# The last feed-forward product of a one-core encoder kernel, as seven Strassen block products instead of eight plain ones

## The chip, the core and the metric

The kernel runs on one core of one Trainium2 chip, in float32. The metric is the time of one execution on the device in microseconds (us); less is better. TensorE multiplies, VectorE (DVE in the rows), ScalarE (ACT) and GpSimd (POOL) do the elementwise work, and transfers between HBM and the core's memory are issued by queues: SyncE (SP) issues the weight loads and the stores, GpSimd a few others.

## The reference

One encoder layer on 512 tokens of width 1024 (no loop over layers: `DEPTH` is 1): three token mixers, their gated sum, and a gated feed-forward network. What matters here is the end:

```python
x = x + merged @ w_out[l]
h = rmsnorm(x, norm_ffn[l])
gu = h @ ffn_w_gate_up[l]                    # 1024 -> 2 * 2816
x = x + (silu(gu[..., :D_FF]) * gu[..., D_FF:]) @ ffn_w_down[l]   # 2816 -> 1024
return rmsnorm(x, final_norm)
```

## The kernel before, in words

The program is written by hand, one instruction stream for each engine, with semaphores between them; no scheduler moves anything. A float32 product is made from three faster ones: every operand is rounded to a `hi` part (by ScalarE, type float32r), the rest `lo` = operand - `hi` is made by VectorE, and `product` (lines 913 to 915) issues `hi*hi`, `hi*lo` and `lo*hi` into the same PSUM bank. A bank holds 128x512 results; there are eight.

Weights come in blocks in the order of the list `weight_blocks`, each up to 128 x 2048 elements (1 MB). A block passes three stages: SyncE loads it into one of three `w_raw` buffers (line 681, after `w_lo_done` says that the block three ahead has been split), ScalarE rounds it into one of two `w_hi` buffers once TensorE has used the block two ahead (`consumed`), and VectorE writes the rest into `w_lo` (line 1998 is VectorE's tensor_tensor helper, line 1544 ScalarE's activation helper). On ScalarE and VectorE this preparation is the call `prep(after(block))` at the place where TensorE works on `block`: it prepares the next one.

The stages around the change, in order of time:

- the gates and branch products, 12 + 12 blocks, from about 450 to 648; then `merged @ w_out`, four blocks `("wo", half, kk)`. GpSimd issues one transfer for the residual `x1` when the last branch block is done (line 893); VectorE's `residual` waits for it (`x1_landed`) and stands ahead of the preparation of the fourth `w_out` block.
- gate and up, 22 blocks `("gu", f)` for 128 features each, 48 matmuls a block. The weight is the stationary operand, `hT_hi` and `hT_lo` the moving one. ScalarE takes silu of the gate bank, VectorE multiplies it with the up bank, in PSUM; ScalarE rounds the result to `act_hi` and VectorE writes `act_lo`.
- the last product, 12 blocks `("down", half, f0)`: for each half of 512 output columns, over 22 feature tiles f, four token tiles t. The activation is stationary (128x128), the weight moves (512 columns). A half fills four banks, so the second half's products run while VectorE adds the first half into `x1` (`add_glu`).
- the tail: ScalarE sums squares of each 512 columns of `x1`, VectorE makes the reciprocal root, GpSimd multiplies `x1` with the final norm's weights (line 902), ScalarE and VectorE scale two token tiles each, SyncE stores.

GpSimd has nothing to do between the scan's last operation (`r_tok`, line 829) and the `x1` transfer but wait.

## Time and profile before

| | |
|---|---|
| median of 3 runs | 1077.66 us (1075.33 to 1756.04) |
| the profiled execution | 1073.17 us |
| its span, first to last instruction | 1071.4 us |
| granted TensorE clock, mean over the span | 0.992 of full |
| TensorE busy | 1036.9 us (97%) |
| VectorE busy | 521.4 us (49%) |
| ScalarE busy | 379.2 us (35%) |
| GpSimd busy | 138.1 us (13%) |
| moved by transfers | 87.18 MB, 81 GB/s over the span |

Busy time is the sum of an engine's instructions. TensorE's matmuls overlap each other, so the length of one is not the interval between two. The second part of the page cuts the span into 40 slices of 26.8 us; each digit is a share in tenths. The profile attributes an idle stretch to what ended it ("<-PE psum" is: the semaphore came from a matmul that wrote psum). "The order" below is the list of an engine's instructions as they stand in the program, with no times in it.

### The profile page before, as it was taken

What the parts mean: (1) busy time and instruction counts of PE and PEld (TensorE: products, weight loads), DVE (VectorE), ACT (ScalarE), POOL (GpSimd) and SP (SyncE); (2) the same over time, 40 slices, a digit from 0 to 9 for tenths busy, and PEclk for the clock granted to TensorE, in tenths of its full rate; (3) what the DMA queues carried; (4) which work ended last, traced back from release to release, by engine and by line L of the source; (5) the groups of instructions that cost most, each with busy time, mean ns of one, the idle gap of its engine ahead of it and who ended that gap; (6) DMA issues with size and microseconds to landing.
All of it is one profiled execution on the core that took longest, in us unless ns stands there. A gap on an engine that the chain in (4) does not pass through costs nothing.

```text
span 1071.4 us, 14260 instructions
## 1 busy us (share of the span) xinstructions
PE 1036.9 (97%) x5850; PEld 863.5 (81%) x5850; DVE 521.4 (49%) x731; ACT 379.2 (35%) x567; POOL 138.1 (13%) x208
## 2 busy tenths in 40 slices
PE   8999999999989998999999999899999999999995
PEld 6889889866678887888888888788888888888884
DVE  6775546477666778455152525543233333322313
ACT  6545645754432221633232312343232322221312
POOL 4010001436763221000000000000000000000201
PEclk9999999999999999999999999999999999999998
DMA  9431230000100014123232336222433333233201
GB/s 301 132 109 58 79 98 2 1 4 9 21 12 2 2 40 133 45 76 102 78 118 86 95 118 214 79 79 79 115 82 108 89 97 100 83 114 116 87 13 79
DMA packets 101856, 87.18 MB, mean 81 GB/s; under 512 B 12117, under 2 KB 90401, under 8 KB 101792
## 3 DMA queue, kind: packets, MB, share of 16 engines
q1 hardware_dynamic: 100144, 81.80, 25.2%
q0 software_dynamic: 1488, 4.40, 1.1%
q8 instruction: 47, 0.77, 0.3%
q14 instruction: 17, 0.14, 0.0%
q10 hardware_dynamic: 160, 0.07, 0.0%
HBM read 83.64 MB, written 2.62 MB: 81 GB/s over the span
## 4 chain that ended last, share of the span: by engine, by line
PE 93%; DVE 4%; issue 1%; ACT 1%; DMA 1%; POOL 0%; SPq 0%; DVEq 0%; POOLq 0%; ACTq 0%
PE psum L913 24%; PE psum L914 24%; PE psum L915 24%; PE psum L1232 2%; PE psum L1239 1%; PE psum L1252 1%; PE psum L1331 1%; PE psum L1387 1%; PE psum L1206 1%; PE psum L1375 1%; PE psum L1304 1%; PE psum L1361 1%; PE psum L1192 1%; PE psum L1126 1%; DVE Xm L1998 1%
## 5 line engine op out<-in xcount | busy, mean ns | idle before, releaser
L1998 DVE TENSOR_TENSOR w_lo<-w_raw,w_hi 128x2048 fp32r<-128x2048 f32 (+3 forms) x81 | 166.9, 2060 | 232.2 <-ACT w_hi L1544 232.1
L913 PE MATMUL psum<-hT_hi,w_hi 128*128 128x512 f32 x704 | 275.2, 391 | 1.0 <-DVE hT_lo L2042 1.0
L914 PE MATMUL psum<-hT_lo,w_hi 128*128 128x512 f32 x704 | 274.4, 390 | 0.0
L915 PE MATMUL psum<-hT_hi,w_lo 128*128 128x512 f32 x704 | 274.2, 390 | 0.0
L1544 ACT ACTIVATE w_hi<-w_raw 128x2048 fp32r<-128x2048 f32 (+3 forms) x82 | 140.8, 1718 | 159.7 <-PE psum L915 147.5
L913 PEld LDWEIGHTS psum<-hT_hi,w_hi 128*128 128x128 f32 x704 | 132.6, 188 | 28.7 <-issue 1.2
L915 PEld LDWEIGHTS psum<-hT_hi,w_lo 128*128 128x128 f32 x704 | 132.4, 188 | 27.5
L914 PEld LDWEIGHTS psum<-hT_lo,w_hi 128*128 128x128 f32 x704 | 132.4, 188 | 27.3
L1998 DVE TENSOR_TENSOR psum<-gate_act,psum 128x512 f32<-128x512 f32 x22 | 15.3, 696 | 120.4 <-PE psum L915 120.4
L913 PE MATMUL psum<-w_hi,act_hi 128*128 128x512 f32 x176 | 68.5, 389 | 0.0
L914 PE MATMUL psum<-w_lo,act_hi 128*128 128x512 f32 x176 | 68.5, 389 | 0.0
L915 PE MATMUL psum<-w_hi,act_lo 128*128 128x512 f32 x176 | 68.5, 389 | 0.0
L1544 ACT ACTIVATE act_hi<-psum 128x512 fp32r<-128x512 f32 x22 | 13.2, 600 | 122.6 <-DVE psum L1998 122.6
L2088 DVE SCALAR_TENSOR_TENSOR dnT<-psum,vcol,dnT 128x510 f32<-128x510 f32 (+1 forms) x48 | 35.9, 749 | 13.6 <-ACT dnT L1544 12.1
L1544 ACT ACTIVATE p_tok<-psum,smax 128x512 f32<-128x512 f32 (+1 forms) x48 | 29.5, 615 | 32.7 <-DVE smax L2321 24.6
L1544 ACT ACTIVATE sig<-psum 128x512 f32<-128x512 f32 x24 | 14.0, 599 | 76.3 <-PE psum L915 76.3
L915 PEld LDWEIGHTS psum<-w_hi,act_lo 128*128 128x128 f32 x176 | 33.0, 188 | 6.9
L913 PEld LDWEIGHTS psum<-w_hi,act_hi 128*128 128x128 f32 x176 | 33.0, 188 | 6.9
L914 PEld LDWEIGHTS psum<-w_lo,act_hi 128*128 128x128 f32 x176 | 33.0, 188 | 6.7
L896 POOL DMA_DIRECT2D fin_w<-in_final_norm_dram x1 | 0.5, 541 | 291.9 <-PE psum L915 291.9
L913 PE MATMUL psum<-oT_hi,w_hi 128*128 128x512 f32 x96 | 37.3, 389 | 0.0
L914 PE MATMUL psum<-oT_lo,w_hi 128*128 128x512 f32 x96 | 37.3, 389 | 0.0
(315 smaller groups left out, 1596.3 us busy)
## 6 DMA issues: line engine op xcount, KB each, us to landing
w_raw<-in_ffn_w_gate_up_dram SPq DMA_DIRECT2D x44, 512.0 KB
w_raw<-in_w_in_dram SPq DMA_DIRECT2D x21, 1024.0 KB
w_raw<-in_ffn_w_down_dram SPq DMA_DIRECT2D x10, 1024.0 KB
w_raw<-in_w_out_dram SPq DMA_DIRECT2D x4, 1024.0 KB
x_tok<-in_x_dram SPq DMA_DIRECT2D x4, 512.0 KB, 5.1
w_raw<-in_mem_w_kv_dram SPq DMA_DIRECT2D x2, 1024.0 KB
w_raw<-in_w_branch_mla_dram SPq DMA_DIRECT2D x4, 512.0 KB
w_raw<-in_w_branch_dn_dram SPq DMA_DIRECT2D x4, 512.0 KB
```

The costliest lines, as they stand in the source:

```text
L913: pe.matmul(o, s_hi, m_hi, start=first, stop=False)
L914: pe.matmul(o, s_hi, m_lo, start=False, stop=False)
L915: return pe.matmul(o, s_lo, m_hi, start=False, stop=last)
L1126: m = pe.transpose(bank(key, QK)[:, j * P:(j + 1) * P], qk_tok[:, t % 2, h * QK:(h + 1) * QK], ident[:, :])
L1192: pe.matmul(bank(key), lhs_rows[q, d, :], rhs_rows[q, d, p, :, :].rearrange("p j n -> p (j n)"), start=True, stop=True).then_inc(full(key), 1)
L1206: m = pe.matmul(bank(key)[:, j * P:(j + 1) * P], dnT[half, 4 + j, t * P:(t + 1) * P], rhs, start=True, stop=True)
L1232: pe.matmul(bank(key), qT[:, h, t * P:(t + 1) * P], kT[:, h, :], start=True, stop=True).then_inc(full(key), 1)
L1239: m = pe.transpose(bank(key)[:, k * P:(k + 1) * P], p_tok[:, n % 2, k * P:(k + 1) * P], ident[:, :])
L1252: m = pe.matmul(out[u * DV:(u + 1) * DV, :], v_mla[:, k, (h0 + u) * DV:(h0 + u + 1) * DV], pT4[(n + u) // 2 % 2][:, (n + u) % 2, k * P:(k ...
L1544: return nc.scalar.activation(o, i, f, **kw)
L1998: return dve.tensor_tensor(o, a, b, op)
L2088: ins = dve.scalar_tensor_tensor(out=dnT[:, ct, a:b], in0=bank(key)[:, a + s:b + s], scalar=vcol[:, c:c + 1], in1=dnT[:, ct, a:b], op0=ALU ...
```

## The change

Cut the activations A (512 tokens x 2816 features) and the weights W (2816 x 1024) into halves: A11, A12 / A21, A22 and W11, W12 / W21, W22. Eight block products make A @ W. Strassen's form makes it with seven (M1 to M7) from sums and differences of quarters; every factor is a quarter, or a sum or difference of two quarters, and VectorE adds or subtracts the seven products into `x1`.

- **Product.** 22 steps instead of 12 blocks. A step s < 11 takes feature tiles i and i + 11 and does four products (M1, M4, M7, M5) of 256 x 128 x 512, 24 matmuls; a step s >= 11 does three (M2, M3, M6), 18 matmuls. The last two steps go product by product, not step by step. Each M has two banks. The second three use banks 0 to 5, those of M1, M4 and M7.
- **Weight quarters.** Of the seven factors two are plain quarters, one is a difference made by VectorE in the loaded buffer (`step_difference`), and four are sums `w_sum` that exist in HBM: GpSimd copies all of `ffn_w_down` (11.53 MB) to `w_sum` with four transfers HBM to HBM, waits for them, then adds quarters to it with eight transfers that accumulate into their destination, 1.44 MB each. SyncE waits for all eight before the first step's load.
- **Activations.** They are no longer split as they come: VectorE writes the product of gate and up in float32 to `acts`, GpSimd makes five differences for each pair of feature tiles (`pair_sums`), ScalarE rounds four or three factors a step to one of three `a_hi` buffers, VectorE writes `a_lo`. The second and third of these buffers lie on `hT_hi` and `hT_lo`, so they can be written only after the last gate/up product.
- **Order.** Gate/up tiles come as 0, 11, 1, 12, ... (`GU_ORDER`). The final adds are `take(m, row, half, op, step)`: each bank is added to or subtracted from one or two quarters of `x1`, 24 adds instead of 8. GpSimd's final-norm load moves ahead in its queue (`fin_w` lies on used activations).

The core of the diff:

```diff
+NP = NF // 2
+GU_ORDER = [i + NP * u for i in range(NP) for u in range(2)]
+STEPS = 2 * NP
+FINAL = [(half, 2 * row + t) for half, row in ((0, 0), (0, 1), (1, 0), (1, 1)) for t in range(2)]
+SUM_PARTS = 8
+FIRST_FOUR, LAST_THREE = (1, 4, 7, 5), (2, 3, 6)
...
+        acts = v("acts", [P, NP, 7, 256], 0)
+        sums_at = [(v0 + 77 * KB), hbase + 12 * KB, hbase + 20 * KB]
+        a_hi = [at(f"a_hi{i}", [P, 4, 256], F32R, o) for i, o in enumerate(sums_at)]
+        a_lo = [at(f"a_lo{i}", [P, 4, 256], F32R, o + 4 * KB) for i, o in enumerate(sums_at)]
+        dw = [at(f"dw{i}", [P, 4, 512], F32, ring + 8 * KB * ((len(blocks) + i) % RAW)) for i in range(RAW)]
+        late = lambda i: acts[:, i, 3:7, :].rearrange("p a b -> p (a b)")
+        y_out = [late(t) for t in range(NT)]
+        fin_w, square4 = late(NT), late(NT + 1)
...
+        def step_in(s):
+            return (w_hi[(NB + s) % 2], w_lo[(NB + s) % 2], a_hi[s % 3], a_lo[s % 3])
+
+        def step_landed(eng, s):
+            eng.wait_ge(dw_landed[s % 3], 16 * sum(3 if i < NP else 2 for i in range(s % 3, s + 1, 3)))
+
+        def step_free(eng, s):
+            if s < 2:
+                filled(eng, ("u", GU_ORDER[NF - 2 + s]))
+            elif s - 2 == NP - 1:
+                filled(eng, ("M", FIRST_FOUR[-1], 1))
+            else:
+                eng.wait_ge(step_used, s - 1 - (s - 2 > NP - 1))
+
+        factors = lambda s: 4 if s < NP else 3
...
+            upper, lower = (slice(0, D_FF // 2), slice(D_FF // 2, D_FF))
+            left, right = slice(0, 512), slice(512, D)
+            in_steps = lambda a, r: a[r, :].rearrange("(i p) n -> i p n", p=P)
+            w_top, w_low = in_steps(ffn_w_down[0], upper), in_steps(ffn_w_down[0], lower)
+            s_top, s_low = in_steps(w_sum, upper), in_steps(w_sum, lower)
+            sp.wait_ge(sum_ready, 16 * SUM_PARTS)
+            for s in range(STEPS):
+                if s < RAW:
+                    sp.wait_ge(w_lo_done, NB - RAW + 1 + s)
+                else:
+                    sp.wait_ge(dw_lo, s - RAW + 1)
+                i, slot, landed = s % NP, dw[s % 3], dw_landed[s % 3]
+                sp.dma_start(slot[:, 0, :], w_top[i, :, left]).then_inc(landed, 16)
+                if s < NP:
+                    sp.dma_start(slot[:, 3, :], w_low[i, :, right]).then_inc(landed, 16)
+                pair = (s_low if s < NP else s_top)[i, :, :].rearrange("p (u n) -> p u n", u=2)
+                sp.dma_start(slot[:, 1:3, :], pair).then_inc(landed, 16)
...
+            for c in range(4):
+                r = slice(D_FF // 4 * c, D_FF // 4 * (c + 1))
+                pool.dma_start(w_sum[r, :], ffn_w_down[0][r, :]).then_inc(sum_begun, 16)
+            pool.wait_ge(sum_begun, 16 * 4)
+            for c in range(SUM_PARTS // 4):
+                top = slice(D_FF // 4 * c, D_FF // 4 * (c + 1))
+                low = slice(D_FF // 2 + top.start, D_FF // 2 + top.stop)
+                left, right = slice(0, 512), slice(512, D)
+                for dst_r, dst_c, src_r, src_c in ((low, left, top, left), (low, right, low, left), (top, left, top, right),
+                                                   (top, right, low, right)):
+                    pool.dma_start(w_sum[dst_r, dst_c], ffn_w_down[0][src_r, src_c], accum_op=ALU.add).then_inc(sum_ready, 16)
+
             consumed(pool, index[("br", 3, 2)])
             pool.dma_start(x1[:, :, :], x[0].rearrange("(t p) d -> p t d", p=P)).then_inc(x1_landed, 16)
 
-            consumed(pool, index[("gu", NF - 1)])
...
+            def pair_sums(i):
+                for u in range(2):
+                    released(pool, ("u", i + NP * u))
+                a = lambda n: acts[:, i, n, :]
+                pool.tensor_tensor(a(4), a(0), a(3), ALU.subtract).then_inc(act_sums, 1)
+                pool.tensor_tensor(a(5), a(1), a(0), ALU.subtract).then_inc(act_sums, 1)
+                pool.tensor_tensor(a(6), a(1), a(3), ALU.subtract).then_inc(act_sums, 1)
+                pool.wait_ge(act_sums, 5 * i + 3)
+                pool.tensor_tensor(a(1), a(2), a(3), ALU.subtract).then_inc(act_sums, 1)
+                pool.wait_ge(act_sums, 5 * i + 4)
+                pool.tensor_tensor(a(2), a(2), a(0), ALU.subtract).then_inc(act_sums, 1)
+
+            for i in range(NP):
+                pair_sums(i)
+            pool.wait_ge(a_lo_done, NT + 1)
+            pool.dma_start(fin_w, final_norm.partition_broadcast(P)).then_inc(fin_landed, 16)
...
+            def down_product(s, m, a_unit, w_unit):
+                wh, wl, ah, al = step_in(s)
+                c = slice(512 * w_unit, 512 * w_unit + 512)
+                first, last = s % NP == 0, s % NP == NP - 1
+                for t in range(2):
+                    key = ("M", m, t)
+                    if first:
+                        claim(pe, key)
+                    r = slice(t * P, (t + 1) * P)
+                    ins = product(bank(key), ah[:, a_unit, r], al[:, a_unit, r], wh[:, c], wl[:, c], first, last)
+                    if last:
+                        ins.then_inc(full(key), 1)
+                return ins
+
+            def step_ready(s):
+                pe.wait_ge(dw_lo, s + 1)
+                pe.wait_ge(a_lo_done, s + 1)
+
+            for s in range(STEPS - 2):
+                step_ready(s)
+                for m, a_unit, w_unit in ((1, 1, 0), (4, 0, 1), (7, 3, 2), (5, 2, 3)) if s < NP else ((2, 1, 0), (3, 0, 2), (6, 2, 1)):
+                    ins = down_product(s, m, a_unit, w_unit)
+                if s != NP - 1:
+                    ins.then_inc(step_used, 1)
+            for m, a_unit, w_unit in ((2, 1, 0), (3, 0, 2), (6, 2, 1)):
+                for s in (STEPS - 2, STEPS - 1):
+                    if m == 2:
+                        step_ready(s)
+                    down_product(s, m, a_unit, w_unit)
...
+            def step_rounded(s):
+                wh, _, _, _ = step_in(s)
+                n = factors(s)
+                step_free(act, s)
+                step_landed(act, s)
+                if s < NP:
+                    act.wait_ge(dw_diff, s + 1)
+                A(wh[:, 0:512 * n], dw[s % 3][:, 0:n, :].rearrange("p a b -> p (a b)")).then_inc(dw_hi, 1)
...
+            for s in range(1, STEPS):
+                step_rounded(s)
+                if s == 1:
+                    acts_rounded(s)
+                acts_rounded(s + 1)
...
+            def step_difference(s):
+                if s < NP:
+                    step_landed(dve, s)
+                    d = dw[s % 3]
+                    tt(d[:, 0, :], d[:, 0, :], d[:, 3, :], ALU.subtract).then_inc(dw_diff, 1)
+
+            def acts_rest(s):
+                _, _, ah, al = step_in(s)
+                n, first = factors(s), 3 if s < NP else 0
+                dve.wait_ge(a_hi_done, s + 1)
+                tt(al[:, 0:n, :], acts[:, s % NP, first:first + n, :], f32(ah[:, 0:n, :]), ALU.subtract).then_inc(a_lo_done, 1)
+
+            def step_rest(s):
+                wh, wl, _, _ = step_in(s)
+                n = factors(s)
+                dve.wait_ge(dw_hi, s + 1)
+                tt(wl[:, 0:512 * n], dw[s % 3][:, 0:n, :].rearrange("p a b -> p (a b)"), f32(wh[:, 0:512 * n]),
+                   ALU.subtract).then_inc(dw_lo, 1)
...
+            for s in range(1, STEPS):
+                if s == NP + 1:
+                    take(1, 0, 0, ALU.add, x1_added)
+                    take(1, 1, 1, ALU.add, None)
+                    taken(1)
+                    take(4, 0, 0, ALU.add, x1_added)
+                    take(4, 1, 0, ALU.add, None)
+                    taken(4)
+                    take(7, 0, 0, ALU.add, None)
+                acts_rest(s)
+                step_difference(s + 1)
+                step_rest(s)
+                if s == NP + 2:
+                    taken(7)
+                    take(5, 0, 0, ALU.subtract, x2_ready)
+                if s == NP + 3:
+                    take(5, 0, 1, ALU.add, None)
+            taken(5)
+            take(2, 1, 0, ALU.add, x2_ready)
+            take(2, 1, 1, ALU.subtract, None)
+            taken(2)
+            take(3, 0, 1, ALU.add, x2_ready)
+            take(3, 1, 1, ALU.add, None)
+            taken(3)
+            take(6, 1, 1, ALU.add, x2_ready)
             final_means(0)
```

Three places of the order, row by row as it is printed. First VectorE at the turn from gate and up to the last product, before (`w_lo0` and `w_lo1` are the two buffers, numbers behind names are memory locations; a block of weights is 128x2048, the fifth of a half 128x2048 and the sixth 128x1024):

```order
L1998 TENSOR_TENSOR psum<-gate_act_56,psum 128x512 [waits bank_free2,bank_full3]
L1998 TENSOR_TENSOR act_lo_165<-psum,act_hi_164 128x512 [waits glu_hi]
L1998 TENSOR_TENSOR w_lo0_87<-w_raw1_83,w_hi0_85 128x2048 [waits w_hi_done]
L1998 TENSOR_TENSOR w_lo1_88<-w_raw2_84,w_hi1_86 128x2048 [waits w_hi_done]
L1998 TENSOR_TENSOR w_lo0_87<-w_raw0_82,w_hi0_85 128x2048 [waits w_hi_done]
L1998 TENSOR_TENSOR w_lo1_88<-w_raw1_83,w_hi1_86 128x2048 [waits w_hi_done]
L1998 TENSOR_TENSOR w_lo0_87<-w_raw2_84,w_hi0_85 128x1024 [waits w_hi_done]
```

and now (`dw0` to `dw2` are the loaded steps, `a_lo` the rests of the activations; the first four rows behind the first `acts` belong to steps 0 and 1):

```order
L2102 TENSOR_TENSOR acts_164<-gate_act_56,psum 128x2x256 [waits bank_free0,bank_full1]
L2102 TENSOR_TENSOR dw0_171<-dw0_171 128x512 [waits dw_landed0]
L2102 TENSOR_TENSOR dw1_172<-dw1_172 128x512 [waits dw_landed1]
L2102 TENSOR_TENSOR a_lo0_168<-acts_164,a_hi0_165 128x1024 [waits a_hi_done]
L2102 TENSOR_TENSOR w_lo1_88<-dw0_171,w_hi1_86 128x2048 [waits dw_hi]
L2102 TENSOR_TENSOR acts_164<-gate_act_56,psum 128x2x256 [waits bank_free2,bank_full3]
L2102 TENSOR_TENSOR a_lo1_169<-acts_164,a_hi1_166 128x1024 [waits a_hi_done]
L2102 TENSOR_TENSOR dw2_173<-dw2_173 128x512 [waits dw_landed2]
L2102 TENSOR_TENSOR w_lo0_87<-dw1_172,w_hi0_85 128x2048 [waits dw_hi]
L2102 TENSOR_TENSOR a_lo2_170<-acts_164,a_hi2_167 128x1024 [waits a_hi_done]
L2102 TENSOR_TENSOR dw0_171<-dw0_171 128x512 [waits dw_landed0]
L2102 TENSOR_TENSOR w_lo1_88<-dw2_173,w_hi1_86 128x2048 [waits dw_hi]
```

Ahead of each step's weight rest there now stand the rest of its activations and the difference of the next step, and the last gate/up product (the second `acts` row) stands between the work of step 0 and that of step 1. Second, VectorE in the middle of the product, where banks are emptied while TensorE goes on into others, before:

```order
L1998 TENSOR_TENSOR w_lo1_88<-w_raw0_82,w_hi1_86 128x2048 [waits w_hi_done]
L1998 TENSOR_TENSOR x1_161<-x1_161,psum 128x512 [waits bank_full0]
L1998 TENSOR_TENSOR x1_161<-x1_161,psum 128x512 [waits bank_full1]
L1998 TENSOR_TENSOR x1_161<-x1_161,psum 128x512 [waits bank_full2]
L1998 TENSOR_TENSOR x1_161<-x1_161,psum 128x512 [waits bank_full3]
L1998 TENSOR_TENSOR w_lo0_87<-w_raw1_83,w_hi0_85 128x2048 [waits w_hi_done]
```

and now, behind the weight rest of step 11:

```order
L2102 TENSOR_TENSOR x1_161<-x1_161,psum 128x512 [waits bank_full0]
L2102 TENSOR_TENSOR x1_161<-x1_161,psum 128x512 [waits bank_full1]
L2102 TENSOR_TENSOR x1_161<-x1_161,psum 128x512 [waits bank_full0]
L2102 TENSOR_TENSOR x1_161<-x1_161,psum 128x512 [waits bank_full1]
L2102 TENSOR_TENSOR x1_161<-x1_161,psum 128x512 [waits bank_full2,bank_free1,bank_free0]
L2102 TENSOR_TENSOR x1_161<-x1_161,psum 128x512 [waits bank_full3]
L2102 TENSOR_TENSOR x1_161<-x1_161,psum 128x512 [waits bank_full2]
L2102 TENSOR_TENSOR x1_161<-x1_161,psum 128x512 [waits bank_full3]
L2102 TENSOR_TENSOR x1_161<-x1_161,psum 128x512 [waits bank_full4,bank_free3,bank_free2]
L2102 TENSOR_TENSOR x1_161<-x1_161,psum 128x512 [waits bank_full5]
L2102 TENSOR_TENSOR a_lo0_168<-acts_164,a_hi0_165 128x768 [waits a_hi_done]
L2102 TENSOR_TENSOR w_lo1_88<-dw0_171,w_hi1_86 128x1536 [waits dw_hi]
```

Four adds with a 2048-column rest on either side have become ten, ahead of the activations' rest and the weight rest of step 12. Third, GpSimd's queue behind the scan, before:

```order
L829 TENSOR_TENSOR r_tok<-v_tok,dg 128x512 [waits bank_full7]
L829 TENSOR_TENSOR r_tok<-v_tok,dg 128x512 [waits bank_full4]
L893 DMA x_161<-in_x_dram 128x4x1024 [waits bank_full7]
L896 DMA fin_w<-in_final_norm_dram 128x1024 [waits bank_full3]
L902 TENSOR_TENSOR y_out<-x_161,fin_w 128x512 [waits x2_ready,fin_landed]
L902 TENSOR_TENSOR y_out<-x_161,fin_w 128x512 [waits x2_ready] x7
```

and now:

```order
L875 TENSOR_TENSOR r_tok<-v_tok,dg 128x512 [waits bank_full7]
L875 TENSOR_TENSOR r_tok<-v_tok,dg 128x512 [waits bank_full4]
L940 DMA w_sum<-in_ffn_w_down_dram 64x11264 x4
L948 DMA w_sum<-in_ffn_w_down_dram 704x512 [waits sum_begun]
L948 DMA w_sum<-in_ffn_w_down_dram 704x512 x7
L951 DMA x_161<-in_x_dram 128x4x1024 [waits bank_full7]
L957 TENSOR_TENSOR acts<-acts 128x256 [waits bank_free3,bank_free1]
L958 TENSOR_TENSOR acts<-acts 128x256
L959 TENSOR_TENSOR acts<-acts 128x256
L961 TENSOR_TENSOR acts<-acts 128x256 [waits act_sums]
L963 TENSOR_TENSOR acts<-acts 128x256 [waits act_sums]
```

The twelve new transfers and the wait between them stand between the scan and the transfer of `x1`, in the same queue; the copies are described as 64 rows of 11264 elements, the sums as 704 rows of 512.

## Rows read from the trace of the kernel before

**Rows 1.** The page, parts 1 and 2: busy time, and the granted clock.

```profile
PE 1036.9 (97%) x5850; PEld 863.5 (81%) x5850; DVE 521.4 (49%) x731; ACT 379.2 (35%) x567; POOL 138.1 (13%) x208
...
PEclk9999999999999999999999999999999999999998
```

**Rows 2.** The page, part 5: group | busy us, mean ns | idle before.

```profile
L913 PE MATMUL psum<-w_hi,act_hi 128*128 128x512 f32 x176 | 68.5, 389 | 0.0
```

**Rows 3.** Timeline of TensorE: start us, length us, engine, line, operation; last product.

```profile
951.46 0.39 PE L913 MATMUL psum<-w_hi,act_hi 128*128 128x512 f32 x1
...
1060.03 0.39 PE L915 MATMUL psum<-w_hi,act_lo 128*128 128x512 f32 x1
```

**Rows 4.** Windows: stretch, its length, busy time per engine, PEclk, DMA share, GB/s.

```profile
core 0: us, PE busy (x) PEld busy (x) DVE busy (x) ACT busy (x) POOL busy (x), PEclk, DMA share, GB/s
...
697.00:935.00 238.00, 238.00 (x1051) 197.65 (x1050) 84.58 (x72) 70.75 (x73) 0.00 (x0) 0.99 0.33 93
935.00:1056.00 121.00, 121.00 (x536) 100.19 (x535) 27.21 (x18) 24.72 (x23) 7.65 (x5) 1.00 0.22 74
```

**Rows 5.** Timelines of ScalarE and VectorE at the second block of the last product.

```profile
951.72 1.92 ACT L1544 ACTIVATE w_hi<-w_raw 128x2048 fp32r<-128x2048 f32 x1 [7.81 <-PE psum L915]
...
953.67 2.29 DVE L1998 TENSOR_TENSOR w_lo<-w_raw,w_hi 128x2048 fp32r<-128x2048 f32 x1 [7.43 <-ACT w_hi L1544]
```

**Rows 6.** Groups by form, 400 to 1072: VectorE, then ScalarE.

```profile
L1998 DVE TENSOR_TENSOR w_lo<-w_raw,w_hi 128x2048 fp32r<-128x2048 f32 x50 | 114.6, 2292 | 135.3 <-ACT w_hi L1544 135.3
L1998 DVE TENSOR_TENSOR w_lo<-w_raw,w_hi 128x1024 fp32r<-128x1024 f32 x14 | 17.2, 1226 | 80.2 <-ACT w_hi L1544 80.2
...
L1998 DVE TENSOR_TENSOR x<-x,psum 128x512 f32<-128x512 f32 x16 | 10.7, 684 | 17.0 <-PE psum L915 17.0
...
L1544 ACT ACTIVATE w_hi<-w_raw 128x2048 fp32r<-128x2048 f32 x50 | 95.5, 1910 | 122.4 <-PE psum L915 110.2 <-DVE attT L1998 12.2
L1544 ACT ACTIVATE w_hi<-w_raw 128x1024 fp32r<-128x1024 f32 x14 | 14.8, 1058 | 33.7 <-PE psum L915 33.7
```

**Rows 7.** Groups by form of GpSimd, whole span.

```profile
L902 POOL TENSOR_TENSOR y_out<-x,fin_w 128x512 f32<-128x512 f32 x8 | 12.2, 1544 | 108.7 <-DVE x L1998 108.5
...
L800 POOL TENSOR_TENSOR block_in<-block_fb 128x256 f32<-128x256 f32 x2 | 1.7, 853 | 0.2
```

**Rows 8.** Timeline of VectorE in the tail.

```profile
1060.46 0.69 DVE L1998 TENSOR_TENSOR x<-x,psum 128x512 f32<-128x512 f32 x1 [0.60 <-PE psum L915]
1061.07 0.16 DVE L2029 RECIPROCAL small<-small 128x2 f32<-128x2 f32 x1
1061.26 1.45 DVE L1998 TENSOR_TENSOR small<-small 128x2 f32<-128x2 f32 x2
...
1063.64 0.36 DVE L1998 TENSOR_TENSOR small<-small 128x2 f32<-128x2 f32 x2
```

**Rows 9.** Timeline of GpSimd: its last operations of the scan.

```profile
406.14 2.48 POOL L829 TENSOR_TENSOR r_tok<-v_tok,dg 128x512 f32<-128x512 f32 x2
```

**Rows 10.** Windows: the stretch in which `x1` and a block of w_out land.

```profile
650.00:655.00 5.00, 5.00 (x24) 4.14 (x23) 3.17 (x3) 2.06 (x2) 0.00 (x0) 1.00 1.04 400
```

**Rows 11.** Timeline of GpSimd, then issues: KB each, us from issue to landing.

```profile
648.27 0.83 POOL L893 DMA_DIRECT2D x<-in_x_dram  x1 [239.66 <-PE psum L915]
...
x<-in_x_dram POOLq DMA_DIRECT2D x1, 2048.0 KB, 11.0
```

**Rows 12.** Transfers issued: KB each, us from issue to landing.

```profile
mem_tok<-in_mem_dram POOLq DMA_DIRECT2D x1, 1024.0 KB, 6.2
```

**Rows 13.** Timeline of the queue of SyncE, 405 to 430.

```profile
406.25 19.86 SPq L681 DMA_DIRECT2D w_raw<-in_w_in_dram  x4
```

**Rows 14.** Timelines of VectorE and ScalarE at the first gate block.

```profile
444.95 2.28 DVE L1998 TENSOR_TENSOR w_lo<-w_raw,w_hi 128x2048 fp32r<-128x2048 f32 x1
...
450.89 1.91 ACT L1544 ACTIVATE w_hi<-w_raw 128x2048 fp32r<-128x2048 f32 x1
```

**Rows 15.** Timelines of ScalarE and VectorE at the blocks of w_out.

```profile
658.95 1.92 ACT L1544 ACTIVATE w_hi<-w_raw 128x2048 fp32r<-128x2048 f32 x1 [6.89 <-PE psum L915]
...
671.78 2.29 DVE L1998 TENSOR_TENSOR w_lo<-w_raw,w_hi 128x2048 fp32r<-128x2048 f32 x1 [1.32 <-ACT w_hi L1544]
```

152 lines of the change are left out of this document (68 added, 84 removed).

## The prediction

> **What bounds the kernel now.** I read the page first: TensorE has work for 97% of the span at a granted clock of full level [rows 1], so every microsecond saved must come out of TensorE's own work or its two ends. The groups of the page then give the last product: 176 products of three matmuls each (528), 128x512 [rows 2]. In the timeline the first matmul of the second block starts at 951.46 and the last of the product at 1060.03 [rows 3]: 479 intervals, 0.2267 us each; the 0.39 us of a row is a length with overlap and is not used as a price. With the first block's 48 ahead of it the stage runs from 940.58 to 1060.26: 119.7 us with no gap. The windows show how idle the others are there: VectorE 27 us and ScalarE 25 us of 121, DMA share 0.22 [rows 4]. So the product is a pure TensorE stage with wide cover, and the work that the change adds lands on VectorE, ScalarE, GpSimd and DMA.
>
> **Part 1, fewer matmuls.** Seven block products x 11 steps x 2 row tiles x 3 = 462 matmuls instead of 528. Removed: 66 x 0.2267 = **-15.0 us**. That is 1.4%: it is the most that the change can give.
>
> **Part 2, the cadence of a step.** A step of the first half has 24 matmuls (5.44 us), one of the second half 18 (4.08 us); before, a block had 48 (10.88 us). Weight rounding is double buffered, so ScalarE may start step s when TensorE leaves step s-2. The same handover stands in the trace: TensorE begins a block at 951.46 [rows 3], ScalarE 951.72, VectorE 953.67, done 955.96 [rows 5]. By size: VectorE 2.29 us for 2048 columns, 1.23 for 1024, 0.68 for 512; ScalarE 1.91 and 1.06 [rows 6]. Between them I interpolate: 1536 columns 1.76 and 1.48, 768 columns 0.96 and 0.84. Hence, from the start of step s-1: first half 0.26 + 1.95 + 2.29 + 0.1 = 4.6 of 5.44 us; second half 0.26 + 1.5 + 1.76 + 0.1 = 3.6 of 4.08. VectorE's total per step is 1.23 + 0.69 + 2.29 = 4.2 of 5.44 us. The steady steps cost TensorE nothing, with 0.8 and 0.5 us to spare. Without double buffering every step would pay 3.6 to 4.6 us. At four joints the cover is gone:
>
> - **Start.** The second activation buffer lies on hT, which the last gate/up block still reads. So after that block ScalarE rounds weights of step 1, then its activations (0.26 + 1.91 + 1.06 = 3.2), and VectorE, which has the activation rest ahead of the weight rest, ends at 3.2 + 1.23 + 0.69 + 2.29 = 7.4; TensorE needs it at 5.44: 2.1 us with the handover. GpSimd's last five 128x256 operations (about 0.85 each [rows 7]) run at the same time. Two 128x2 operations of VectorE took 1.45 us beside GpSimd's final products, and 0.36 after them [rows 8], so I add 0.4: **+2.5 us**. The Trainium skill ("SBUF — State Buffer", the three doors to SBUF) states that a VectorE operation with two SBUF inputs and a GpSimd operation that reads SBUF exclude each other for whole instructions; these rows agree.
> - **Middle.** From the start of step 10: VectorE is free at 3.6 (rest of step 11), then has ten adds some 0.62 apart (0.68 long [rows 6], and the operation behind one starts 0.61 later [rows 8]) before anything of step 12. M1's banks free at 5.4 and 6.1, just in time; M4's first at 8.0, wanted at 5.44 + 1.36 = 6.8: 1.2 us. The adds end at 9.9, the rests of step 12 (0.9 + 1.7) at 12.5; TensorE leaves step 11 at 10.7: 1.8 us. **+3.0 us.**
> - **End.** The last two steps are taken product by product. TensorE needs step 21 after six matmuls (1.36 us) of step 20, while its rounding may start only at step 20's start: 3.6 - 1.36 = **+2.2 us**.
> - **Tail.** Before, VectorE adds the last tile at 1060.46, 0.2 us after TensorE's end [rows 8]. Now ten adds come in the last 5.4 us (10 x 0.62 = 6.2 plus handovers), and the mean of the first two tiles stands behind the last add, not ahead of it: **+1.1 us**. GpSimd's six late products (1.54 each by the mean [rows 7]) end under 5 us after TensorE, about when the last scaling wants them.
>
> GpSimd's 11 x 5 sums (about 4 us per 21.8 us pair of gate/up blocks) are hidden. ScalarE and VectorE lose 22 roundings and 22 rests of the activations under the gate/up blocks; they were hidden too, so nothing is gained.
>
> **Part 3, the sums in HBM.** GpSimd reaches them at about 408.6 [rows 9]: it copies 11.53 MB HBM to HBM, then adds 11.53 MB. Nothing of this kind is in the trace. Nearest rows for the rate: 400 GB/s at DMA share 1.04 with 2 and 4 KB pieces [rows 10], and 93 at 0.33, that is 280 at a full share, with 0.5 KB pieces [rows 4]. Copy: 29 us at 400, 58 us if read and write each cost. Sums: 58 us at 200, 115 us at 100. So they end between about 497 and 583. They are queued ahead of x1's transfer on the same queue, which starts at 648.3 [rows 11]; and step 0's load wants them only some 30 us before 940. I take **0** for the likeliest; the bounds are in the rivals. The Trainium skill ("Collectives: The Full Stack", why ReduceScatter is half of AllGather) says that an adding transfer needs two source reads and runs at half rate. By it the sums take 58 to 115 us; nothing here shows it yet.
>
> **Part 4, loads of the steps.** 1.05 MB per 5.44 us is 193 GB/s, under 400. A slot's next load is issued when its rest is done; its difference and the next rest (3.0 us) must follow within two steps, so it may take 10.9 - 3.0 = 7.9 us. 1 MB landed in 6.2 us [rows 12]: 0.
>
> **Sum.** -15.0 + 2.5 + 3.0 + 2.2 + 1.1 = **-6.2 us**. The profiled execution has 1073.2 us around its span of 1071.4, so 1067.0 for such an execution. The median of the runs shown is 1077.66, 4.5 above it, so I forecast **1071.5**.
>
> **Rivals.**
> - **A, weights starve behind the copy.** Four weight loads are issued between 406 and 426 [rows 13], the copy from 409 in pieces of 45 KB (64x11264 in the order). The first gate block must have landed by 446: VectorE prepared it at 444.95, ScalarE began the next block's at 450.89, 0.26 after TensorE's turn [rows 14]. If the weights got nothing until 468, it would land near 473 and be ready 4.5 later: 27 us late. It is nothing if the copy ends in about 35 us or the weights get 1.3 MB in 36 us, that is 36 GB/s. Also, during the sums, weights need 96 GB/s and 93 at share 0.33 [rows 4] means that they want a third of the engines; a lower share costs up to 10 us. Time 1075 to 1099, middle 1085. Against it: the loads have 13 us or more of slack each. The Trainium skill ("DMA: Bandwidth & Descriptors", arbitration) says that an engine alternates between queues packet by packet; with 45 KB against 1 KB pieces that favours this rival, and no run here shows it. Chance 0.20.
> - **B, the adding transfers are slow (the other side).** x1 comes behind them. VectorE must end the fourth w_out block's rest by TensorE's turn at 680.4 (21.7 after the turn behind ScalarE's row of 658.95); before it stand four adds and the rest itself (before: rest at 671.78; both in [rows 15]), so x1 must land by 675.5 and, at 11.0 us [rows 11], start by 664.5, 16 us later than now. From a copy end of 439 to 468 the sums have 196 to 225 us: it decides from under 51 to 59 GB/s. Each us more is a us of TensorE. At 45 GB/s: 256 us, late by about 60 us, 1130. Nearest rows speak against it by more than 3 times. Chance 0.10.
> - **C, the joints cost little** (VectorE passes the ten adds faster than TensorE needs banks, hand-overs overlap): -12 to -15, 1064. The order puts the adds ahead of step 12's rest, which speaks against. Chance 0.12.
> - **D, the step loads bind.** If a load takes L over 7.9 us, a step takes (L + 3.0) / 2: at 9.5 us 0.8 us more on each of 11: 1080. Chance 0.06.
> - The forecast itself: 0.52, own range 1066 to 1076. That the change does not do what it says is left out: the order shows 462 matmuls.
>
> **Numbers.** The likeliest is 1071.5. The range takes C's low end and A's to 1096; left out are B, A's last part and C's last part, under 0.2. About 2% (21.5 us) is what a measurement of this kernel can tell from no change. Faster by that is beyond the 15 us removed: 0.01. Slower by that: B 0.10 and the upper part of A 0.03, 0.13. Within: 0.86.
>
> **What would show it.** After: TensorE's last product in some 113 us from its first matmul to its last (104.7 of work, 7.7 of waits), with waits only in the second, the twelfth and thirteenth and the last step, released by VectorE's w_lo and adds. A gap of TensorE between 446 and 500 with VectorE's w_lo late and ScalarE waiting for a DMA is A. A wait for x near 680 is B. Waits in every first-half step, ended by a DMA, are D. The prediction is wrong if the stage before 940 changes by more than 2 us, or if steady steps wait.

## The result, and the profile after

The changed kernel takes 1086.2 us (median of 6 runs, 1082.62 to 1612.62), the kernel before 1076.7 us, measured beside it; the ratio is 1.0097 with a 95% interval of 1.0071 to 1.0122. I had forecast 1071.5, some 6 us less than before. It is 9.5 us more: inside my range and under 2%, but on the other side of no change. (Of each kernel's six runs the slowest, 1612.62 at a granted clock of 0.597 and 1756.04, is left out of the ratio.)

| | before | after |
|---|---|---|
| median of 6 runs | 1076.7 us | 1086.2 us |
| span of the profiled execution | 1071.4 us | 1084.4 us |
| matmuls | 5850 | 5784 |
| last product, first matmul to end | 119.7 us | 113.3 us |
| GpSimd's `r_tok` to the issue of `x1`'s transfer | 242.1 us | 257.9 us |

The page of the kernel after, parts 1 and 2:

```profile
PE 1030.5 (95%) x5784; PEld 854.8 (79%) x5784; DVE 567.8 (52%) x768; ACT 403.2 (37%) x577; POOL 209.2 (19%) x275
...
PE   8999999999989998699999999989999999999994
...
PEclk9999999999999999989999999989999999999998
DMA  8431230000100019999642326323333333336461
```

The 66 matmuls are gone. But TensorE's row now has a 6, the clock's an 8 beside it, and under them DMA is full for four slices (before the change TensorE's clock stands at 9 there [rows 1]). A slice is 27 us, so this is the stretch from about 407 to 515, in which the copy and most of the adding transfers of Part 3 run. TensorE's timeline after, the waits that the timeline of before does not have (in brackets: us idle ahead, and what ended it):

```profile
461.31 0.80 PE L984 MATMUL psum<-hT_hi,w_hi 128*128 128x512 f32 x1 [8.85 <-DVE w_lo L2102]
...
528.24 0.50 PE L984 MATMUL psum<-hT_hi,w_hi 128*128 128x512 f32 x1 [2.23 <-DVE w_lo L2102]
...
967.00 0.50 PE L984 MATMUL psum<-w_hi,a_hi 128*128 128x512 f32 x1 [2.66 <-DVE w_lo L2102]
...
1023.99 0.50 PE L984 MATMUL psum<-w_hi,a_hi 128*128 128x512 f32 x1 [0.85 <-DVE x L2102]
1028.50 0.50 PE L984 MATMUL psum<-w_hi,a_hi 128*128 128x512 f32 x1 [1.45 <-DVE w_lo L2102]
...
1065.09 0.50 PE L984 MATMUL psum<-w_hi,a_hi 128*128 128x512 f32 x1 [2.01 <-DVE w_lo L2102]
```

The last four are the joints of Part 2. The first two are new, and both lie beside the transfers of Part 3. `product` is lines 984 to 986 now, the helpers of VectorE and ScalarE 2102 and 1627.

**The big gap, followed back.** The timelines of GpSimd and of SyncE's queue:

```profile
408.49 2.47 POOL L875 TENSOR_TENSOR r_tok<-v_tok,dg 128x512 f32<-128x512 f32 x2
...
410.90 2.06 POOL L940 DMA_DIRECT2D w_sum<-in_ffn_w_down_dram  x4
450.44 9.16 POOL L948 DMA_DIRECT2D w_sum<-in_ffn_w_down_dram  x8 [37.47 <-DMA w_sum<-in_ffn_w_down_dram]
...
411.67 0.39 SPq L710 DMA_DIRECT2D w_raw<-in_w_in_dram  x1
```

The timelines of ScalarE and of VectorE:

```profile
452.31 1.91 ACT L1627 ACTIVATE w_hi<-w_raw 128x2048 fp32r<-128x2048 f32 x1 [13.72 <-DMA w_raw<-in_w_in_dram]
454.24 1.28 ACT L1627 ACT_TABLE_LOAD   x1
...
455.64 1.13 ACT L1627 ACTIVATE square<-o_tok 128x512 f32<-128x512 f32 x2
...
456.39 2.66 DVE L2608 TENSOR_REDUCE small<-square 128x8 f32<-128x512 f32 x4 [14.19 <-ACT square L1627]
458.97 2.28 DVE L2102 TENSOR_TENSOR w_lo<-w_raw,w_hi 128x2048 fp32r<-128x2048 f32 x1
```

The copy ran from 410.90 to no later than 450.44. The load of the gate block, 1 MB, was issued 0.8 us behind it (411.67) and was usable at 452.31, after 40.6 us; a transfer of that size landed in 6.2 us elsewhere [rows 12]. ScalarE rounded the block in 1.9 us, but VectorE had its reduction of the squares first in its order, and ScalarE makes the squares behind that rounding: 4.7 us pass from the end of the rounding (454.22) to the start of `w_lo` (458.97). TensorE starts at 461.31, 9.0 us after the block was usable. In the kernel before the same order stands, but the block was there long before, so all of it was done in time (timelines of ScalarE and VectorE):

```profile
436.39 1.90 ACT L1544 ACTIVATE w_hi<-w_raw 128x2048 fp32r<-128x2048 f32 x1
...
442.37 2.67 DVE L2504 TENSOR_REDUCE small<-square 128x8 f32<-128x512 f32 x4 [2.26 <-ACT square L1544]
```

**Why the load took so long.** The profile's view of the transfers counts what each of the two queues moved, here from 432 to 440: q0 is GpSimd's (the copy), q1 SyncE's (the weights); packets, MB, share of the 16 engines' time.

```profile
DMA packets 149, 2.78 MB, mean 348 GB/s; under 512 B 14, under 2 KB 89, under 8 KB 89
...
q0 software_dynamic: 74, 2.70, 100.2%
q1 hardware_dynamic: 75, 0.08, 4.0%
```

Both queues had nearly the same number of packets served. But 60 of the copy's 74 are over 8 KB (2.70 MB in 60 is 45 KB each), and the weights' have 1 KB, so in 8 us the weights got 0.08 MB: 10 GB/s.

**What the clock adds.** Windows of the kernel after (columns as in [rows 4]):

```profile
430.00:435.00 5.00, 5.00 (x34) 4.52 (x34) 0.00 (x0) 3.08 (x4) 0.00 (x0) 1.00 1.06 353
450.00:455.00 5.00, 2.46 (x11) 1.69 (x9) 0.00 (x0) 2.67 (x2) 4.57 (x7) 1.00 1.09 361
455.00:460.00 5.00, 0.00 (x0) 0.00 (x0) 3.50 (x5) 2.98 (x6) 4.60 (x5) 0.70 1.12 236
460.00:465.00 5.00, 3.69 (x9) 2.92 (x10) 4.43 (x13) 3.14 (x5) 0.00 (x0) 0.50 1.13 212
465.00:470.00 5.00, 5.00 (x19) 4.04 (x18) 4.81 (x4) 4.87 (x3) 0.00 (x0) 0.77 1.11 231
500.00:505.00 5.00, 5.00 (x24) 4.13 (x23) 2.52 (x3) 1.05 (x2) 0.00 (x0) 1.00 1.11 231
530.00:535.00 5.00, 5.00 (x19) 4.01 (x19) 2.29 (x1) 1.91 (x1) 0.00 (x0) 0.79 0.27 93
```

While TensorE stands still its clock falls to 0.50, the 1.2 GHz level, and stays there after it starts again; its timeline shows matmuls 0.43 us apart (before: 0.23):

```profile
461.90 0.63 PE L985 MATMUL psum<-hT_lo,w_hi 128*128 128x512 f32 x1
462.33 0.63 PE L986 MATMUL psum<-hT_hi,w_lo 128*128 128x512 f32 x1
...
467.37 0.40 PE L986 MATMUL psum<-hT_hi,w_lo 128*128 128x512 f32 x1
467.61 0.39 PE L984 MATMUL psum<-hT_hi,w_hi 128*128 128x512 f32 x1
```

From 461.31 to 467.61 there are 15 intervals in 6.3 us, where 3.4 would do at 0.2267: 2.9 us lost. Behind the second gap the clock reads 0.87 (525 to 530) and 0.79 (530 to 535), which is 5 x 0.13 + 5 x 0.21 = 1.7 us; the intervals say the same (ten from 528.24 to 532.22 take 3.98 us where 2.27 would do). So the stage lost 8.85 + 2.9 + 2.23 + 1.7 = 15.7 us. GpSimd's rows give the same from outside: from `r_tok` to the issue of `x1`'s transfer 242.13 us before (406.14 [rows 9] to 648.27 [rows 11]), and 257.94 after (408.49 to 666.43), 15.8 more:

```profile
666.43 0.83 POOL L951 DMA_DIRECT2D x<-in_x_dram  x1 [206.83 <-PE psum L986]
```

From there to the start of the last product both kernels take 292.3 us. With a front of the kernel 2.35 us longer in this execution (408.49 against 406.14), the last product 6.4 us shorter and the tail 1.2 us longer: 2.35 + 15.8 - 6.4 + 1.2 = 13.0, the difference of the spans.

### The profile page after: what moved, and what is told of

Same layout as the page of the kernel before. It is cut to its first block and busy times, and to the rows that moved or that the text cites. A ratio compares the mean times of both kernels' runs of the same rounds, so it can differ in the third digit from the quotient of the medians.

```text
span 1084.4 us, 14328 instructions
## 1 busy us (share of the span) xinstructions
PE 1030.5 (95%) x5784; PEld 854.8 (79%) x5784; DVE 567.8 (52%) x768; ACT 403.2 (37%) x577; POOL 209.2 (19%) x275
## 5 line engine op out<-in xcount | busy, mean ns | idle before, releaser
L984 PE MATMUL psum<-hT_hi,w_hi 128*128 128x512 f32 x704 | 277.0, 394 | 12.0 <-DVE w_lo L2102 11.1
L2102 DVE TENSOR_TENSOR w_lo<-w_raw,w_hi 128x2048 fp32r<-128x2048 f32 (+3 forms) x69 | 142.7, 2068 | 161.2 <-ACT w_hi L1627 161.2
L1627 ACT ACTIVATE w_hi<-w_raw 128x2048 fp32r<-128x2048 f32 (+3 forms) x70 | 119.8, 1711 | 200.9 <-PE psum L986 165.3
L2102 DVE TENSOR_TENSOR acts<-gate_act,psum 128x512 f32<-128x512 f32 x22 | 15.1, 688 | 142.2 <-PE psum L986 142.2
L984 PE MATMUL psum<-w_hi,a_hi 128*128 128x512 f32 x154 | 60.6, 393 | 7.0 <-DVE w_lo L2102 6.1
L986 PE MATMUL psum<-w_hi,a_lo 128*128 128x512 f32 x154 | 60.0, 389 | 0.0
L985 PE MATMUL psum<-w_lo,a_hi 128*128 128x512 f32 x154 | 60.0, 389 | 0.0
L1627 ACT ACTIVATE w_hi<-dw 128x2048 fp32r<-128x2048 f32 (+1 forms) x22 | 37.5, 1703 | 59.9 <-PE psum L986 54.6
L2102 DVE TENSOR_TENSOR w_lo<-dw,w_hi 128x2048 fp32r<-128x2048 f32 (+1 forms) x22 | 45.7, 2079 | 21.6 <-ACT w_hi L1627 21.6
L984 PEld LDWEIGHTS psum<-w_hi,a_hi 128*128 128x128 f32 x154 | 28.9, 188 | 15.3 <-DVE w_lo L2102 7.8
L1627 ACT ACTIVATE gate_act<-psum 128x512 f32<-128x512 f32 x22 | 13.2, 598 | 73.5 <-PE psum L986 73.5
```

What stands on the lines that cost most here:

```text
L984: pe.matmul(o, s_hi, m_hi, start=first, stop=False)
L985: pe.matmul(o, s_hi, m_lo, start=False, stop=False)
L986: return pe.matmul(o, s_lo, m_hi, start=False, stop=last)
L1627: return nc.scalar.activation(o, i, f, **kw)
L2102: return dve.tensor_tensor(o, a, b, op)
```

## Experiments

The theory: the last product does what it was changed for, and the loss is contention. The transfers of Part 3 take the DMA engines from the weight loads of the gate stage; the copy starves them by its 45 KB pieces, and the adding transfers starve them a little by their load. The rivals: the loss is only that of queueing more on GpSimd or SyncE, or it is in the new last product. All eight kernels ran beside the kernel before (4 to 10 runs each), which took 1073.29 us in the first four comparisons and 1073.12 in the last four, so ratios compare better than microseconds across the two. In every profile I read the length from `r_tok` to `x1`'s transfer, called **the stage** here (before 242.1, after 257.9).

### Without the sums: e1_no_sums

The copies and adding transfers are left out, and the steps load plain quarters in place of sums (so the output lacks the sums). Everything in the last product stays.

```diff
-            s_top, s_low = in_steps(w_sum, upper), in_steps(w_sum, lower)
-            sp.wait_ge(sum_ready, 16 * SUM_PARTS)
+            s_top, s_low = w_top, w_low
...
-            for c in range(4):
-                r = slice(D_FF // 4 * c, D_FF // 4 * (c + 1))
-                pool.dma_start(w_sum[r, :], ffn_w_down[0][r, :]).then_inc(sum_begun, 16)
...
```

> Leaves out the copy and all eight adding transfers; the steps load the plain quarters of ffn_w_down in the places of w_sum, so the product is another one with the same work on every engine. My theory (the late weight loads under the copy and the sums cost 15.8 us, two gaps and the slow clock behind them; the rest of the change gains what was forecast): no gap between 450 and 540, x1 issued near 648 to 650, time about 1070, 6 us under before, last product still 113 us. Rival (the joints, the 22 smaller steps or the changed gate/up stage cost the time): 1080 or more, with x1's transfer at its old place and the loss behind it.

Measured: 1068.86 us, ratio 0.9955 (0.9929 to 0.998). Stage 241.9 us, no gap in it; the waits of the last product are the same four, 6.1 us behind `w_lo` and 0.85 behind the adds. All of the loss is in the twelve transfers, and the last product alone is worth 4.4 us.

### The copy alone: e2_copy_only

The copy stays, the adding transfers are left out (the output lacks them).

```diff
-            sp.wait_ge(sum_ready, 16 * SUM_PARTS)
+            sp.wait_ge(sum_begun, 16 * 4)
...
-                    pool.dma_start(w_sum[dst_r, dst_c], ffn_w_down[0][src_r, src_c], accum_op=ALU.add).then_inc(sum_ready, 16)
```

> Keeps the four copies HBM to HBM and leaves out the eight adding transfers, so w_sum holds plain weights. My theory: the first gap (8.9 us, near 452 to 461, and about 3 us of slow clock) is the copy's and stays; the second (2.2 us near 526) is the sums' and goes: time about 1082. Rival (both gaps come from the sums, whose issue at 450 coincides with the first): no gap, about 1070.

Measured: 1080.56 us, ratio 1.0067 (1.0044 to 1.009). ScalarE's timeline:

```profile
449.82 1.91 ACT L1619 ACTIVATE w_hi<-w_raw 128x2048 fp32r<-128x2048 f32 x1 [13.17 <-DMA w_raw<-in_w_in_dram]
```

TensorE's gap of 8.30 us is there, the second is not; the stage takes 253.2 us. The copy costs 11.7 us against e1 (11.3 of the stage), and the adds the rest, 4.7 us of the stage (257.9 against 253.2).

### The copy in small pieces: e3_copy_2kb

The same bytes and the same adds, but each copy is split in column halves, so that a row of it is 2 KB and the transfer can no longer be cut into pieces of 45 KB. (I expected pieces of 2 KB; by the counts below they are of 4 KB, two rows each.)

```diff
-                pool.dma_start(w_sum[r, :], ffn_w_down[0][r, :]).then_inc(sum_begun, 16)
-            pool.wait_ge(sum_begun, 16 * 4)
+                for h in (slice(0, 512), slice(512, D)):
+                    pool.dma_start(w_sum[r, h], ffn_w_down[0][r, h]).then_inc(sum_begun, 16)
+            pool.wait_ge(sum_begun, 16 * 8)
```

> All as in the changed kernel, but the copy is made by eight transfers of column halves, in pieces of 2 KB instead of 45 KB; same bytes. If an engine serves whole pieces by turns and the 45 KB pieces starve the 1 KB pieces of the weights: the first gate block lands by 440 instead of 452, no first gap, about 1075. If the weights only lose to the bytes in flight: landing stays near 450, first gap within 2 us of 8.9, time 1086.

Measured: 1075.34 us, ratio 1.0021 (0.9999 to 1.0044). The timelines of ScalarE and GpSimd:

```profile
441.04 1.90 ACT L1628 ACTIVATE w_hi<-w_raw 128x2048 fp32r<-128x2048 f32 x1
...
413.22 5.46 POOL L941 DMA_DIRECT2D w_sum<-in_ffn_w_down_dram  x8
460.63 9.20 POOL L949 DMA_DIRECT2D w_sum<-in_ffn_w_down_dram  x8 [41.95 <-DMA w_sum<-in_ffn_w_down_dram]
```

The copy is still running when the gate block is rounded at 441.04 with no wait for a load; it takes 47.4 us from its issue, where the changed kernel's takes 39.5. The DMA engines are as full as in the changed kernel (share 1.04 from 430 to 435, 1.00 from 450 to 455). What the queues moved from 428 to 436:

```profile
q0 software_dynamic: 602, 2.37, 79.7%
q1 hardware_dynamic: 602, 0.60, 22.9%
```

Again both queues had equal numbers of packets served, but with 4 KB (2.37 MB in 602) against 1 KB the weights got 0.60 MB in 8 us, 75 GB/s instead of 10. So it is not how full the engines are that kept the weights out but how large a piece stands ahead of each of theirs. The Trainium skill ("DMA: Bandwidth & Descriptors", Queues, rings and completion order) says that a DMA engine turns between the queues packet by packet; the equal counts in both runs agree, and the changed kernel's 40.6 us is what it can cost. What remains, a stage of 247.3 us (5.2 over before), lies beside the adds: waits of 2.27 us at 519 and 0.69 us at 532 behind `w_lo`, whose rounding waits for a load each time (6.56 and 10.58 us of ScalarE). The adds' pieces are of 2 KB, but there are as many of them as of the weights': in the changed kernel, from 451 to 525, 5694 packets of theirs and 5828 of the weights, which moved 5.85 MB, 79 GB/s. The same work moves 84 GB/s in the kernel before (449 to 523), so here the weights fall behind by little.

### The transfers paced: e4_paced

The copy in eight parts, each behind one gate block, and the eight adding transfers one by one behind the gate/up pairs. Nothing is left out.

```diff
-            for c in range(4):
-                r = slice(D_FF // 4 * c, D_FF // 4 * (c + 1))
+            for k in range(8):
+                consumed(pool, index[("gate", k // 2, 2 * (k % 2))])
+                r = slice(D_FF // 8 * k, D_FF // 8 * (k + 1))
...
+                if i < SUM_PARTS:
+                    add_quarters(i)
```

> Same transfers, placed apart: the copy in eight pieces of 1.44 MB, each behind a gate block that TensorE has finished (two in each of the four column blocks), and one adding transfer of 1.44 MB behind each of the first eight pairs of gate/up tiles. My theory: each piece takes the 16 engines for 5 to 10 us, less than the 13 us of slack of a weight load, so no load is late: no gap, about 1070, as without the sums. Rival (any overlap with HBM writes makes loads late, or an adding transfer alone lasts longer than the slack): gaps behind the pieces, 1075 or more.

Measured: 1068.94 us, ratio 0.9961 (0.9935 to 0.9986). The stage takes 242.1 us, as before the change, without a gap. It equals the kernel without the transfers (0.9955): spread out they cost nothing that shows, though the copy's pieces are as large. The issues of the copy and of the adds (KB each, median us from issue to landing):

```profile
w_sum<-in_ffn_w_down_dram POOLq DMA_DIRECT2D x8, 1408.0 KB, 6.5
w_sum<-in_ffn_w_down_dram POOLq DMA_DIRECT2D x8, 1408.0 KB, 12.3
```

A part of the copy had landed after 6.5 us, and TensorE waited for no weight block of the stage. GpSimd's queue holds more transfers here than in the changed kernel, and SyncE's the same ones, so queueing more is not what costs.

### The transfers alone: e8_before_with_sums

The kernel before with its last product as it was, and the twelve transfers added at the place where the change has them; nobody reads what they make.

```diff
+            for c in range(4):
+                r = slice(D_FF // 4 * c, D_FF // 4 * (c + 1))
+                pool.dma_start(w_sum[r, :], ffn_w_down[0][r, :]).then_inc(sum_begun, 16)
+            pool.wait_ge(sum_begun, 16 * 4)
...
+                    pool.dma_start(w_sum[dst_r, dst_c], ffn_w_down[0][src_r, src_c], accum_op=ALU.add).then_inc(sum_ready, 16)
```

> The kernel before, its last product as it was, with nothing added but the twelve transfers of the change (four copies of 2816 KB and eight adding transfers of 1408 KB, at the same place of the queue); nobody reads the sums, and only the last stores wait for them. My theory, contention in the gate and up stage: the same two gaps as in the changed kernel (8 to 9 us near 453 to 461, 2 us near 526 to 528, each with some microseconds at half the clock behind it), x1's transfer issued about 16 us later, and a time some 16 us over the kernel before, near 1089. Rival, the loss comes of the new order of the last product or of its waits for the sums: less than 5 us over the kernel before.

Measured: 1089.0 us, ratio 1.0153 (1.0128 to 1.0178), 15.9 us over the kernel before. TensorE's timeline:

```profile
461.09 0.79 PE L928 MATMUL psum<-hT_hi,w_hi 128*128 128x512 f32 x1 [8.55 <-DVE w_lo L2013]
...
527.36 0.80 PE L928 MATMUL psum<-hT_hi,w_hi 128*128 128x512 f32 x1 [2.26 <-DVE w_lo L2013]
```

The same two gaps at the same places; stage 257.1 us. The last product is the old one here and nothing but the last stores waits for the sums, so neither the new product nor its wait for the sums is needed for the loss. Together with e1 this closes the account: -0.45% for the product, +1.53% for the transfers make +1.1%, and the change measured +1.0% (0.7 to 1.2).

### The joints of the last product: e5_start, e6_end, e7_both

These start from e4_paced. e5 gives the second activation a buffer that the last gate/up block does not read, and ScalarE rounds it before that block's silu; e6 gives the last step's weights memory of their own; e7 has both.

```diff
-        a_hi = [at(f"a_hi{i}", [P, 4, 256], F32R, o) for i, o in enumerate(sums_at)]
+        a_hi = [at(f"a_hi{i}", [P, 4, 256], F32R, v0 + 85 * KB if i == 1 else o) for i, o in enumerate(sums_at)]
+        end_hi = at("end_hi", [P, 1536], F32R, hbase)
+        end_lo = at("end_lo", [P, 1536], F32R, hbase + 6 * KB)
...
-                step_free(act, s)
+                if s < STEPS - 1:
+                    step_free(act, s)
...
+                    acts_rounded(1)
...
-                if s == 1:
-                    acts_rounded(s)
```

> The paced kernel (1068.94 us, sums spread over the gate and up stage), with the start joint undone: the second activation of the last product has a buffer of its own and ScalarE rounds it in the last gate block, ahead of the silu. My theory: the 2.66 us wait of the last product's first rounding is VectorE's and ScalarE's work for step 1 squeezed behind the last block, so it falls to 0.5 us or less and the kernel gains about 2.3 us, some 1066.6 where the paced one takes 1068.9. Rival: the wait is that of the two-input difference on GpSimd and VectorE's port, or of a load; then 2 us or more of it stay and the time does not move by more than 0.5 us. The waits at the middle (0.9 and 1.5 us) and the end (2.0 us) stay in both.

Measured: 1067.56 us, ratio 0.9946 (0.9926 to 0.9965). That is 1.4 us under the paced kernel's median, where 2.3 was expected. The start's wait falls from 2.66 to 0.37 us, as expected:

```profile
948.76 0.50 PE L990 MATMUL psum<-w_hi,a_hi 128*128 128x512 f32 x1 [0.37 <-DVE w_lo L2107]
```

> The paced kernel with the end joint undone: the last step's two weight tiles lie in memory of their own, so that their rounding need not wait until TensorE has read the tiles of step 19. My theory: the 2.0 us wait at the end falls to about 0.8 us and the kernel gains about 1.2 us, some 1067.7. Rival: the wait is VectorE's own work at the end (the reductions into the output tiles); then it stays at 2 us and the time is that of the paced kernel within 0.3 us. The waits of the start (2.7 us) and the middle (0.9 and 1.5 us) stay in both.

Measured: 1066.44 us, ratio 0.9944 (0.9923 to 0.9966), 2.5 us under the paced kernel where 1.2 was expected. The wait at the end falls from 2.01 to 0.47 us, a little more than expected, 1.5 us for 1.2:

```profile
1047.52 0.50 PE L994 MATMUL psum<-end_hi,a_hi 128*128 128x512 f32 x1 [0.47 <-DVE end_lo L2113]
```

> The paced kernel with both joints undone. My theory: the two gains add up, about 3.5 us below the paced kernel, near 1065.5 us, a ratio to the kernel before of 0.992 to 0.994; of TensorE's waits in the last product those of the middle (0.9 and 1.5 us) and about 0.8 us at the end stay. Rival: what is saved at one joint comes back at another, since ScalarE and VectorE have the same work in sum; then it gains less than 2 us.

Measured: 1064.41 us (1060.02 to 1066.34), ratio 0.9919 (0.9896 to 0.9942). Both waits are gone together (0.37 and 0.47 us) and the middle ones stay (0.86 and 1.46); nothing comes back elsewhere. The waits fell by 3.8 us, the median by 4.5 against the paced kernel. Each of the three intervals overlaps with that of e4, so the times alone do not show the separate gains; the waits in the traces do, and e7's upper bound (0.9942) stands below e4's middle (0.9961). This kernel, 8.7 us under the one before, is the best of the study.

## Why the prediction was wrong

**The step that failed is Part 3, "I take 0 for the likeliest".** It was right about rates and wrong about who gets them. The copy took 39.5 us from its issue (11.53 MB, so 292 GB/s), between my 29 and 58; the adds ran from 450.4 until between 525 and 530, 75 to 80 us (about 150 GB/s), between my 58 and 115; the sums were ready near 528, in my 497 to 583, far ahead of `x1` and step 0. The half rate for adding transfers that I cited from the Trainium skill ("Collectives: The Full Stack", why ReduceScatter is half of AllGather, where it is told of a collective's add) agrees: 150 to 292 is 0.51, and in e4, each beside weight loads, 1408 KB were copied in 6.5 us and added in 12.3, that is 0.53. In both, the pieces of the copy are larger than those of the adds, so how much of the half comes of the pieces is not shown. But I asked when the sums would be ready, and only rival A asked what the weight loads get in the meantime. It was given 0.20, against it "13 us or more of slack each". One load took 40.6 us instead of some 6.

**Rival A was the right mechanism.** It gave two conditions for no loss. One, that the copy ends in about 35 us, was missed in the changed kernel (39.5), but e3 shows that it is not needed: there the copy took 47.4 us and the gate block was in time. The other, that the weights get 36 GB/s, fits both runs: they got 10 in the changed kernel and 75 in e3. With the block usable at 452.31 and "ready 4.5 later" TensorE, which wanted it at 452.46 (461.31 - 8.85), would have waited 4.3 us; it waited 8.85, since it was ready 9.0 us later. What I missed is the order behind the late load: ScalarE's squares and VectorE's reduction, which in the kernel before run under the blocks ahead, stood between. With them it takes 9.0 us from landing to TensorE, so the block had to land by about 441.6 in the kernel before (450.6 - 9.0), not by 446. Its 1085 as the middle came from a wait of 27 us at the far end, so the closeness to 1086.2 is luck. The clock was in no term of the sum at all: 4.6 of the 15.8 us are matmuls at half speed after the two gaps. "During the sums, up to 10 us" was 2.23 + 1.7.

**Part 1** held: 66 matmuls fewer, 0.2267 us each, -15.0.

**Part 2, the joints**, as forecast and measured: start 2.5 and 2.66; middle 1.2 + 1.8 and 0.85 + 1.45; end 2.2 and 2.01; tail 1.1 and 1.2 (before 11.1 from the end of the product to the end of the span, now 12.35). Each of these four waits costs 0.27 us more than its row says, as the critical chain shows, in which a piece lasts from the end of one matmul to the end of the next:

```profile
1028.50 0.50 PE psum L984
1028.99 0.23 PE psum L985
```

The first matmul behind a wait ends 0.50 us after its start, and from there the ends are 0.23 apart. The last product takes 113.3 us, where "some 113" was forecast: 104.7 of work, 7.0 of waits in the rows, 1.1 behind them, and the last 0.5 in intervals a little over 0.2267 (150 matmuls from 1028.50 on have 0.229). With the tail, Parts 1 and 2 gave -6.4 + 1.2 = -5.2 in these profiles, where -6.2 was forecast. That the start and the end were caused by buffers that another block still reads, as Part 2 has it, is shown by e5 and e6. The cause of the middle (the ten adds ahead of step 12's rest) is read from the order and the releasers alone; no run undoes it, so it is not shown. TensorE waited in no steady step, so "0.8 and 0.5 us to spare" was enough. The 0.4 us that I added for GpSimd and VectorE excluding each other has no measurement of its own. GpSimd's and VectorE's timelines in a gate/up pair show the exclusion itself, in a place that costs nothing:

```profile
742.89 0.73 POOL L958 TENSOR_TENSOR acts<-acts 128x256 f32<-128x256 f32 x1
743.58 2.78 POOL L959 TENSOR_TENSOR acts<-acts 128x256 f32<-128x256 f32 x1
...
743.35 2.42 DVE L2102 TENSOR_TENSOR w_lo<-w_raw,w_hi 128x2048 fp32r<-128x2048 f32 x1 [1.32 <-ACT w_hi L1627]
```

GpSimd's operation of 743.58 takes 2.78 us where the one before it took 0.73; it ends at 746.36, 0.6 us after VectorE's.

**Part 4 and the other rivals.** The loads of the steps kept up (4.6 us and 3.0 us to landing); B did not come, since the adds ran at 150 GB/s, not under 59, and D did not. C, cheap joints, is refuted by the four waits. The sum without Part 3, -6.2, has its test in e1 and e4: -4.4 us of medians each, so less than forecast, but the forecast lies within their intervals (-7.6 to -2.1 and -7.0 to -1.5).

**What I said would show it** did: a gap of TensorE between 446 and 500 with VectorE's `w_lo` late and ScalarE waiting for a DMA was to be A, and the prediction wrong "if the stage before 940 changes by more than 2 us". It changed by 15.8.

## What to carry to other kernels

A bulk transfer that is ready long before its reader can still be the most expensive part of a change: price it by what the loads that run beside it get, piece by piece, and look at which of them is wanted first. Cut its pieces or issue it in parts behind consumed blocks, as e4 does at no cost that shows; then of the 15.0 us (1.4%) saved in matmuls 4.4 come through, and giving two of the joints buffers of their own brings it to 8.7. The rest stays in the waits of the middle and in the tail. Where a load comes late, follow the order of every engine behind it, and add matmuls at half clock after the gap.
